# Attention heads of a two-model kernel: one by one, or in pairs on tiles of the matmul array

## The chip, the cores and the metric

One NeuronCore of a Trainium2 chip runs the whole program. Its engines are TensorE (PE, with its weight loads shown as PEld), VectorE (DVE), ScalarE (ACT), GpSimd (POOL) and the queue that issues the transfers (SP). The metric is the device time of one execution in microseconds; the kernel before has a median of 955.63 us over three runs (953.55 to 956.29).

## What is computed

The reference runs two small models on the same 256 tokens of width 1024: a retention layer and a sparse attention layer, then a second block. The change lies in that second block, after its input projection, where two mixers work side by side on 16 meta tokens and 256 real ones. The first is a gated delta rule (4 heads of 128) whose triangular systems are solved in chunks of 16, 128 and 128 tokens. The second is "forgetting" attention, 8 heads of width 64, each of which computes in fp32:

```
c  = cumsum(log_sigmoid(f_raw + f_bias))
sc = q @ k.T * 64**-0.5 + c[:, None] - c[None, :]     # 128 x 144 and 128 x 272 scores
p  = softmax(where(causal, sc, -1e30))
o  = p @ v
```

The outputs of the 256 real tokens alone are needed. Both mixers' outputs (512 columns each) then go through w_out and a SwiGLU layer.

## The kernel before, in words

Weights stream from HBM in units of 1 MB into a ring of four; ScalarE and VectorE split each into a high part (L1643) and a low part (L2082), and the projections take three matmul products of such parts. The mixers' own products (scores, values, triangular solves, transposes) are plain fp32 matmuls, which the trace shows as two passes for each instruction (all but the transposes); all of them are issued from line 776 (`mm`) or from lines of their own.

**The order.** `mixer_order()` is a list written out by hand. TensorE, VectorE and ScalarE each walk through it and do their share of every item, strictly in that order, so it also sets the order in which the four auxiliary PSUM banks are used: each use takes the bank of the use four places earlier (`Banks.open`), and waits until its reader has freed it. Items of the delta rule are `Lz` and `Lx` (level n of the triangular solve of chunk c: a product z and, above level 1, a transpose x; ScalarE copies z, VectorE copies x, and then a product y which VectorE subtracts from the matrix), `W`, and the recurrence over chunks `Vn` (new values), `Vo` (output and state) and `Vg` (norm and gate). GpSimd masks the rows for the next level (L2794) as soon as z of a level is there. `gz` and `mo` are projections with weights; `kv` and `vT` are transposes.

**One head of the forgetting attention** takes four items:
- `Fs`: `fox_scores` multiplies q (128 rows, of which the other head's 64 are zeros) by k, twice (144 and 272 columns), and adds the decay and the causal mask with bf16 products. VectorE takes the maxima (L2575, L2576), ScalarE the exponentials and sums into Pf (L2002), which frees the bank.
- `Fn`: VectorE inverts the sums and scales Pf (L2581, L2584).
- `Ft`: `fox_turn` turns Pf, three transposes of 128 columns (bank fT, copied by ScalarE at L2010) and two of 16 (bank fm, copied by VectorE at L2597).
- `Fo`: `fox_values` multiplies the values of both heads of a pair (128 columns, half of them unused) by the turned Pf in three products of 256, 256 and 128 columns. ScalarE rounds the 64 rows that count (L2015), VectorE subtracts for the low part (L2592), and that frees the bank.

The order puts the eight heads' items between the levels of the solve (`beside[n]`, one list behind the level's `Lz`, one behind its `Lx`), and the last ones (`Fs` of head 7, `Ft` of 6 and 7, `Fo` of 5, 6 and 7) between `W` and `Vn` of chunk 2.

## Time and profile before

| what | value |
|---|---|
| median of three runs | 955.63 us |
| the profiled execution's own time | 952.64 us |
| its span in the trace | 951.1 us |
| TensorE busy | 935.9 us (98%), 6542 passes |
| VectorE busy | 635.5 us (67%) |
| ScalarE busy | 478.5 us (50%) |
| GpSimd busy | 122.0 us (13%) |
| mixers with the attention heads | about 665 to 737 us of the span |

The span runs from the first to the last recorded instruction; the execution's own time is 1.5 us longer. "psum<-R,nw" names what an operation writes and reads: q of heads 0 to 3 lies in nw, of heads 4 to 7 in R; Pf and PfT are the probabilities and their turned form; G (G1 in the program's order), side_sb and PTb belong to the solve. "128*128 128x272 x2" is the part of the array used (rows * columns), the output, and the passes.

### The profile page before, as it was taken

To read this page: it belongs to the slowest core of one execution; us is meant where nothing else is said; L and a number is where in the kernel's file an instruction comes from. 1 tells how busy PE (TensorE), PEld (TensorE's weight loads), DVE (VectorE), ACT (ScalarE), POOL (GpSimd) and SP (SyncE) were. 2 spreads that over 40 slices of the span, in tenths; PEclk is the share of its full clock that TensorE was granted. 3 is DMA by queue.
4 is the path that set the end of the run, shared out by engine and by line. 5 is a ranking of instruction groups with operands and counts; after the bars stand their busy time and mean duration, and the time that the engine had idled before them with its cause. 6 is when DMAs were issued, how large, how long until landed. Compare 5 with 4: busy or idle time off the path is not lost.

```text
span 951.1 us, 16259 instructions
## 1 busy us (share of the span) xinstructions
PE 935.9 (98%) x6542; PEld 835.2 (88%) x6542; DVE 635.5 (67%) x942; ACT 478.5 (50%) x843; POOL 122.0 (13%) x128
## 2 busy tenths in 40 slices
PE   8999999999999999999999999999999999999997
PEld 8988778878998999998888789989788899999885
DVE  5974457566884767678874477988664667666543
ACT  7335446455654554466653556664434554444432
POOL 1000032000320000101310004312320111111001
PEclk9999999999999999999999999999999999999999
DMA  9735435555555863332025453522101555555551
GB/s 326 297 135 187 167 133 177 177 177 177 180 201 209 291 227 134 132 135 89 1 87 180 171 183 134 176 91 89 47 2 45 177 192 186 187 212 178 195 204 44
DMA packets 23518, 150.58 MB, mean 158 GB/s; under 512 B 3564, under 2 KB 3848, under 8 KB 6168
## 3 DMA queue, kind: packets, MB, share of 16 engines
q1 hardware_dynamic: 23104, 149.39, 44.7%
q8 instruction: 52, 0.85, 0.4%
q10 hardware_dynamic: 344, 0.18, 0.1%
q14 instruction: 18, 0.15, 0.1%
HBM read 148.50 MB, written 1.05 MB: 157 GB/s over the span
## 4 chain that ended last, share of the span: by engine, by line
PE 87%; DVE 7%; ACT 3%; issue 1%; DMA 1%; POOL 0%; SPq 0%; ACTq 0%; POOLq 0%; DVEq 0%
PE psum L776 83%; DVE ring_parts L2082 3%; PE psum L857 1%; DVE R L2407 1%; ACT high_parts L1643 1%; ACT R L1828 1%; PE psum L1190 1%; PE psum L1526 1%; DMA h<-in_x 1%; DVE R L2359 1%; DVE PTb_parts L2378 0%; ACT tmp L1681 0%; ACT R L1650 0%; PE psum L1373 0%; DVE nw_parts L2380 0%
## 5 line engine op out<-in xcount | busy, mean ns | idle before, releaser
L2082 DVE TENSOR_TENSOR ring_parts<-ring,high_parts 128x1024 fp32r<-128x1024 f32 (+1 forms) x272 | 333.3, 1264 | 146.4 <-ACT high_parts L1643 145.0
L1643 ACT CAST high_parts<-ring 128x1024 fp32r<-128x1024 f32 x268 | 268.1, 1050 | 185.7 <-PE psum L776 151.8
L776 PE MATMUL psum<-xT_parts,high_parts 128*128 128x256 f32 (+1 forms) x1024 | 228.0, 285 | 1.6 <-DVE ring_parts L2082 1.1
L776 PE MATMUL psum<-xT_parts,ring_parts 128*128 128x256 f32 (+1 forms) x704 | 200.6, 285 | 0.0
L776 PEld LDWEIGHTS psum<-xT_parts,high_parts 128*128 128x128 f32 x1024 | 173.3, 190 | 2.9 <-DVE ring_parts L2082 1.6
L776 PE MATMUL psum<-high_parts,R_parts 128*128 128x512 f32 (+1 forms) x528 | 164.8, 386 | 0.0
L776 PE MATMUL psum<-R_parts,high_parts 128*128 128x256 f32 x832 | 156.0, 277 | 0.0
L776 PE MATMUL psum<-high_parts,xT_parts 128*128 128x512 f32 x480 | 154.3, 397 | 0.0
L776 PEld LDWEIGHTS psum<-xT_parts,ring_parts 128*128 128x128 f32 x704 | 133.3, 189 | 0.1
L776 PEld LDWEIGHTS psum<-R_parts,high_parts 128*128 128x128 f32 x832 | 130.5, 188 | 0.0
L776 PEld LDWEIGHTS psum<-high_parts,R_parts 128*128 128x128 f32 (+1 forms) x528 | 98.7, 188 | 20.5
L776 PEld LDWEIGHTS psum<-high_parts,xT_parts 128*128 128x128 f32 x480 | 89.4, 188 | 20.9 <-issue 1.9
L776 PE MATMUL psum<-ring_parts,xT_parts 128*128 128x512 f32 x256 | 100.6, 393 | 0.0
L776 PE MATMUL psum<-ring_parts,R_parts 128*128 128x512 f32 (+1 forms) x264 | 99.3, 381 | 0.0
L776 PE MATMUL psum<-R_parts,ring_parts 128*128 128x256 f32 x352 | 97.2, 276 | 0.0
L776 PE MATMUL psum<-PTb_parts,high_parts 128*128 128x256 f32 x256 | 73.8, 288 | 0.0
L776 PEld LDWEIGHTS psum<-R_parts,ring_parts 128*128 128x128 f32 x352 | 66.1, 188 | 0.0
L776 PEld LDWEIGHTS psum<-ring_parts,R_parts 128*128 128x128 f32 (+1 forms) x264 | 49.6, 188 | 9.6
L776 PEld LDWEIGHTS psum<-ring_parts,xT_parts 128*128 128x128 f32 x256 | 48.1, 188 | 10.7
L776 PEld LDWEIGHTS psum<-PTb_parts,high_parts 128*128 128x128 f32 x256 | 48.3, 189 | 0.0
L776 PE MATMUL psum<-R 128*128 128x128 f32 (+3 forms) x248 | 47.2, 324 | 0.6 <-DVE R_parts L2592 0.6
L2757 POOL TENSOR_TENSOR R<-R,small 128x1024 f32<-128x1024 f32 x12 | 22.8, 1898 | 194.6 <-DVE small L2354 194.6
(354 smaller groups left out, 1126.4 us busy)
## 6 DMA issues: line engine op xcount, KB each, us to landing
ring<-in_weights SPq DMA_DIRECT2D x135, 1024.0 KB, 4.9
h<-in_x SPq DMA_DIRECT2D x4, 256.0 KB, 4.4
ring<-in_weights SPq DMA_DIRECT2D x4, 256.0 KB, 5.9
ring<-in_weights SPq DMA_DIRECT2D x2, 512.0 KB, 7.4
G<-in_gains SPq DMA_DIRECT2D x2, 512.0 KB, 7.7
out<-xn SPq DMA_DIRECT2D x2, 512.0 KB, 2.6
R<-in_ret_tabs SPq DMA_DIRECT2D x1, 768.0 KB, 13.0
tab<-in_tabs SPq DMA_DIRECT2D x1, 663.5 KB, 6.0
```

Of the source, the lines that this page charges most:

```text
L776: return pe.matmul(out, lhsT, rhs, start=first, stop=last, skip_group_check=True)
L857: ins = pe.transpose(bank[:, k * T + t * P:k * T + (t + 1) * P], src(2 * f + k, t), ident)
L1190: ins = pe.transpose(bank[:, n * P:(n + 1) * P], R[:, c0:c0 + P], ident)
L1526: ins = pe.transpose(bank[0:n, hd * n:(hd + 1) * n], mat(PTb, C_ALL, c, hd), ident[0:n, 0:n])
L1643: act.copy(as_r(hi), value).then_inc(sem("units_high"), 1)
L1828: ins = act.activation(R[:, c0:c0 + n_keys], bank[:, n * n_keys:(n + 1) * n_keys], ACT.Exp, bias=nmx[:, col:col + 1], accum_out=esum[:, co ...
L2082: return dve.tensor_tensor(as_r(value), value, value_of(hi), ALU.subtract)
L2359: main.free(dve.tensor_tensor(two(R[:, R4 + n * 512:R4 + (n + 1) * 512]), two(bank), token_scale2, ALU.mult), key)
L2407: ins = dve.scalar_tensor_tensor(y, raw[:, j, k:k + TM], param("conv_w_2", 12 * k + j), y, ALU.mult, ALU.add)
L2757: pool.tensor_tensor(p, p, spread(esc[:, i * 8:i * 8 + 2 * nh], 1024 // (2 * nh)), ALU.mult).then_inc(sem("nsa_p"), 1)
```

## The change

Heads are handled in pairs. `Fs`, `Fn`, `Ft` and `Fo` have the pair as their key, four of each in place of eight.

- Scores: q and k of one head are read from 64 partitions and not from 128, the two heads' from the lower and the upper half, so each pass takes 64 rows of the array (two row tiles, 64*128). The two heads' products are written in turn, each into a bank of its own; then each head gets its four bf16 products as before.
- Turning: both heads' three large transposes, each into its own bank, and four small ones into one bank. VectorE copies that bank once.
- Values: each product loads 64 columns of values and writes its head's 64 partitions of a common bank (two column tiles, 128*64), the two heads' products in turn. ScalarE and VectorE then handle all 128 partitions at once: four evictions each, where there were eight.
- The order is given anew: the pairs' items stand elsewhere between the levels, and at levels 1 to 3 the side work stands ahead of chunk 0's item and not behind it. `Fs`, `Ft` and `Fo` of the last heads no longer stand inside the recurrence.

```diff
-    beside = {1: ([("Fn", 0), ("vT", 1), ("Fs", 1)], [("vT", 2), ("vT", 0), ("Ft", 0)]), 2: ([("Fn", 1), ("Fs", 2)], [("Fo", 0), ("Ft", 1)]),
...
+              2: ([("Fs", 1)], [("Fo", 0), ("Fn", 1)]),
...
-    order += [("W", 1), ("Fs", 7), ("W", 2), ("Fo", 5), ("Vn", 0), ("Fn", 7), ("Ft", 6), ("Vo", 0), ("gz", 1, 1), ("Vn", 1),
-              ("Fo", 6), ("Ft", 7), ("Vo", 1), ("Fo", 7), ("Vg", 1), ("Vn", 2), ("mo", 0, 0), ("Vo", 2), ("Vg", 2),
...
+        for kind, side_work in zip(("Lz", "Lx"), beside[n]):
+            order += [(kind, n, c) for c in level_chunks(n) if c] + side_work + [(kind, n, c) for c in level_chunks(n) if not c]
+    order += [("W", 1), ("W", 2), ("Ft", 3), ("Vn", 0), ("Fo", 3), ("Vo", 0), ("gz", 1, 1), ("Vn", 1), ("Vo", 1), ("Vg", 1),
...
+            def fox_scores(pair):
+
+                banks = [aux.open(pe, ("fs", 2 * pair + i)) for i in range(2)]
+                k0 = R3 + 4 * TM + pair * TM
+                spans = ((0, P + M), (P + M, 2 * P + M))
+                for b, (c0, n) in enumerate(spans):
+                    for i in range(2):
+                        q = fox_query(2 * pair + i)[head_rows(i), b * P:(b + 1) * P]
+                        mm(banks[i][:, c0:c0 + n], q, R[head_rows(i), k0:k0 + n], b == 0, False)
...
+            def fox_values(pair):
+                wait_read(pe, aux, ("fT", 2 * pair + 1))
+                wait_read(pe, aux, ("fm", pair))
+                bank = aux.open(pe, ("fo", pair))
+                for c, (c0, n, at_) in enumerate(((384, T, 0), (0, T, 0), (T, P, P))):
+                    for i in range(2):
+                        v0 = R3 + 8 * TM + c * 512 + pair * P + i * FD
+                        ins = mm(bank[head_rows(i), at_:at_ + n], R[:, v0:v0 + FD],
+                                 PfT[:, i * 640 + c0:i * 640 + c0 + n], c == 0, c == 2)
+                aux.full(ins, ("fo", pair))
```

The whole list of `beside` is now: level 1, behind `Lz` Fn 0 and vT 1, behind `Lx` vT 2, vT 0 and Ft 0; level 2, Fs 1, then Fo 0 and Fn 1; level 3, gz (0, 0), then Ft 1; level 4, Fs 2, then Fo 1 and Fn 2; level 5, gz (0, 1), then Ft 2; level 6, Fs 3, then Fo 2, gz (1, 0) and Fn 3 (the numbers of F items are pairs). Pair 0's scores stand ahead of kv 0 as head 0's did. The VectorE and ScalarE parts follow the pairs in the same way (two heads' maxima, exponentials and scalings one after the other).

How instructions move, on TensorE at level 2. Before, from one head's scores to the first y products (side_sb,PTb) of the level:

```order
L776 MATMUL psum<-R,nw 128x144 [waits aux_read_by_act]
L776 MATMUL psum<-negc,of_head_3 128x144
L776 MATMUL psum<-causal_b,ident_b 128x128
L776 MATMUL psum<-R,nw 128x272
L776 MATMUL psum<-negc,of_head_3 128x272
L776 MATMUL psum<-causal_b,ident_b 128x128
L776 MATMUL psum<-side_sb,PTb 64x32 [waits aux_read_by_dve,aux_read_by_act]
L776 MATMUL psum<-side_sb,PTb 64x32 x7
L776 MATMUL psum<-side_sb,PTb 64x32 [waits aux_read_by_act,aux_read_by_dve]
L776 MATMUL psum<-side_sb,PTb 64x32 x7
```

Now, from the second head's mask products of pair 1 on:

```order
L774 MATMUL psum<-negc,of_head_3 128x144
L774 MATMUL psum<-causal_b,ident_b 128x128
L774 MATMUL psum<-negc,of_head_3 128x272
L774 MATMUL psum<-causal_b,ident_b 128x128
L774 MATMUL psum<-PTb,R 16x8 [waits aux_read_by_act,aux_read_by_dve,level_part]
L774 MATMUL psum<-PTb,R 16x8 x3
L1528 MATMUL psum<-tab,PTb 16x16 [waits aux_read_by_dve]
L1528 MATMUL psum<-tab,PTb 16x16 x3
L774 MATMUL psum<-side_sb,PTb 64x32 [waits aux_read_by_act,aux_read_by_dve]
L774 MATMUL psum<-side_sb,PTb 64x32 x7
L774 MATMUL psum<-side_sb,PTb 64x32 [waits aux_read_by_act,aux_read_by_dve]
L774 MATMUL psum<-side_sb,PTb 64x32 x7
```

Chunk 0's z and x (R 16x8 and 16x16) now stand between the scores and the y products, and two banks of scores are open where there was one; the first y product is the fourth use behind the first head's scores.

On VectorE, from level 2's subtractions (L2570, now L2573) to level 3's copies of x (L2564, now L2567). Before:

```order
L2570 TENSOR_TENSOR PTb<-PTb,psum 64x4x8x4 [waits aux_filled]
L2570 TENSOR_TENSOR PTb<-PTb,psum 64x4x8x4
L2570 TENSOR_TENSOR PTb<-PTb,psum 16x8x4 [waits aux_filled]
L2592 TENSOR_TENSOR R_parts_56<-psum,R_parts_56 64x256 [waits fox_high,aux_filled]
L2597 COPY PfT<-psum 16x256 [waits aux_filled]
L2564 COPY PTb<-psum 128x512 [waits aux_filled] x2
L2564 COPY PTb<-psum 16x64 [waits aux_filled]
```

Now:

```order
L2573 TENSOR_TENSOR PTb<-PTb,psum 64x4x8x4 [waits aux_filled]
L2573 TENSOR_TENSOR PTb<-PTb,psum 64x4x8x4
L2595 TENSOR_TENSOR R_parts_56<-psum,R_parts_56 128x256 [waits fox_high,aux_filled]
L2585 RECIPROCAL small<-small 128x2 [waits aux_read_by_act]
L2588 TENSOR_SCALAR Pf<-Pf,small 128x144 [waits dve_step]
L2588 TENSOR_SCALAR Pf<-Pf,small 128x272
L2585 RECIPROCAL small<-small 128x2 [waits aux_read_by_act]
L2588 TENSOR_SCALAR Pf<-Pf,small 128x144 [waits dve_step]
L2588 TENSOR_SCALAR Pf<-Pf,small 128x272
L2573 TENSOR_TENSOR PTb<-PTb,psum 16x8x4 [waits aux_filled]
L2567 COPY PTb<-psum 128x512 [waits aux_filled] x2
```

Chunk 0's subtraction (16x8x4) now stands behind the values' eviction and behind the scaling of two heads' probabilities, and so do the copies of x.

## Rows read from the trace of the kernel before

**Rows 1.** Windows: us; busy us and instructions of each engine; TensorE clock; DMA share; GB/s
```profile
690.00:710.00 20.00, 20.00 (x233) 17.13 (x232) 12.25 (x32) 8.01 (x24) 5.00 (x4) 1.00 0.01 2
770.00:800.00 30.00, 30.00 (x267) 30.00 (x266) 20.80 (x24) 14.64 (x17) 3.90 (x3) 1.00 0.55 191
```

**Rows 2.** Waits of TensorE from 664 to 740 us: us in total, times, longest
```profile
PE psum L776 <- DVE R_parts L2592: 0.6, 1, 0.6
PE psum L1452 <- ACT Pf L2002: 0.5, 1, 0.5
...
PE psum L776 <- DVE R L2534: 0.4, 1, 0.4
```

**Rows 3.** Timeline of TensorE, one head's scores and what follows (start us, us)
```profile
669.33 0.41 PE L776 MATMUL psum<-R,nw 128*128 128x144 f32 x2
669.58 0.23 PE L776 MATMUL psum<-negc,of_head 128*128 128x144 bf16 x1
...
669.70 0.68 PE L776 MATMUL psum<-R,nw 128*128 128x272 f32 x2
670.21 0.28 PE L776 MATMUL psum<-negc,of_head 128*128 128x272 bf16 x1
...
670.48 0.30 PE L776 MATMUL psum<-side_sb,PTb 64*64 64x32 f32 x4
```

**Rows 4.** Timeline of TensorE, one head's values and what follows
```profile
701.76 1.25 PE L776 MATMUL psum<-PfT,R 128*128 128x256 f32 x6
702.85 0.49 PE L1373 MATMUL psum<-tab,Pf 128*128 128x128 f32 x3
```

**Rows 5.** Timeline of TensorE in windows of 12 and 15 ns, and one row further on
```profile
666.60 0.27 PE L1335 MATMUL psum<-tab,R 128*16 128x128 f32 x1
666.81 0.24 PE L776 MATMUL psum<-PTb,G 64*64 64x32 f32 x1
...
675.13 0.25 PE L776 MATMUL psum<-PTb,G 64*64 64x32 f32 x2
...
675.72 0.66 PE L1526 MATMUL psum<-tab,PTb 128*128 128x128 f32 x4
```

**Rows 6.** Timeline of all engines, from a head's last score pass to its free bank
```profile
670.33 0.22 PE L776 MATMUL psum<-causal_b,ident_b 128*128 128x128 bf16 x1
...
671.33 0.38 ACT L2002 ACTIVATE Pf<-psum,small 128x144 f32<-128x144 f32 x1 [1.11 <-DVE small L2576]
...
672.42 0.52 PE L1452 MATMUL psum<-tab,tmp 128*128 128x128 f32 x3 [0.54 <-ACT Pf L2002]
```

**Rows 7.** Timeline of VectorE and GpSimd while both work from SBUF, and without GpSimd
```profile
667.62 2.49 POOL L2794 TENSOR_TENSOR G<-PTb,tab 128x512 f32<-128x512 f32 x2 [17.08 <-PE psum L776]
...
667.99 2.29 DVE L2584 TENSOR_SCALAR Pf<-Pf,small 128x144 f32<-128x144 f32 x2
...
677.33 0.56 DVE L2584 TENSOR_SCALAR Pf<-Pf,small 128x144 f32<-128x144 f32 x2
```

**Rows 8.** Timeline of all engines, the state's chain and the gate beside it
```profile
728.04 0.38 PE L776 MATMUL psum<-R,PTb 128*128 128x128 f32 x2
...
729.62 0.69 DVE L2508 SCALAR_TENSOR_TENSOR R<-tmp,R 128x512 f32<-128x512 f32 x1 [2.54 <-ACT tmp L1681]
...
729.82 1.25 PE L776 MATMUL psum<-PfT,R 128*128 128x256 f32 x6
730.02 0.58 ACT L2024 COPY R<-psum 128x512 f32<-128x512 f32 x1 [0.43 <-PE psum L776]
...
734.13 1.25 PE L776 MATMUL psum<-PfT,R 128*128 128x256 f32 x6
...
735.22 0.32 PE L776 MATMUL psum<-R,PTb 128*128 128x128 f32 x1
```

**Rows 9.** Lines by form: the eviction by VectorE of one head's values (count, busy us, mean ns)
```profile
L2592 DVE TENSOR_TENSOR R_parts<-psum,R_parts 64x256 fp32r<-64x256 f32 x8 | 3.4, 421 | 9.3 <-ACT R_parts L2015 7.3 <-PE psum L1377 2.0
```

**Rows 10.** Windows: a stretch in which the granted clock fell
```profile
649.70:653.30 3.60, 3.60 (x20) 3.60 (x19) 3.42 (x9) 0.77 (x1) 0.84 (x2) 0.55 0.00 0
```

More of the change, by code:

```diff
@@ L1380, in fox_values, with head_rows @@
[L1380 to L1393 removed]
+            def head_rows(i):
+                return slice(i * FD, (i + 1) * FD)
@@ new lines, in fox_scores @@
+            def fox_scores(pair):
[7 more added lines that the diff above has]
+                for i in range(2):
+                    hd = 2 * pair + i
+                    for c0, n in spans:
+                        mm(banks[i][:, c0:c0 + n], of_head_3[:, hd:hd + 1].to_broadcast([P, P]), negc[:, 0:n], False, False)
+                        ins = mm(banks[i][:, c0 + n - P:c0 + n], ident_b, causal_b, False, True)
+                    aux.full(ins, ("fs", hd))
@@ new lines, in fox_turn @@
+            def fox_turn(pair):
+                for i in range(2):
+                    hd = 2 * pair + i
+                    pe.wait_ge(sem("fox_scaled"), hd + 1)
+                    bank = aux.open(pe, ("fT", hd))
+                    for n, c0 in enumerate((M, P + 2 * M, 2 * P + 2 * M)):
+                        ins = pe.transpose(bank[:, n * P:(n + 1) * P], Pf[:, i * 416 + c0:i * 416 + c0 + P], ident)
+                    aux.full(ins, ("fT", hd))
+                bank = aux.open(pe, ("fm", pair))
+                for i in range(2):
+                    for n, c0 in enumerate((0, P + M)):
+                        ins = pe.transpose(bank[0:M, i * T + n * P:i * T + (n + 1) * P],
+                                           Pf[:, i * 416 + c0:i * 416 + c0 + M], ident)
+                aux.full(ins, ("fm", pair))
@@ L2006, in _ @@
-                    aux.free(ins, ("fs", hd))
+                    for i in range(2):
+                        hd = 2 * key[0] + i
+                        bank = aux.wait(act, ("fs", hd))
+                        act.wait_ge(sem("fox_max"), hd + 1)
+                        at_ = 0
+                        for b in range(TT):
+                            n = M + (b + 1) * P
+                            c0 = i * 416 + at_
+                            ins = act.activation(Pf[:, c0:c0 + n], bank[:, at_:at_ + n], ACT.Exp,
+                                                 bias=fnm[:, 2 * hd + b:2 * hd + b + 1],
+                                                 accum_out=fsum[:, 2 * hd + b:2 * hd + b + 1])
+                            at_ += n
+                        aux.free(ins, ("fs", hd))
@@ L2007, in _ @@
                 elif kind == "Ft":
-                    hd = key[0]
-                    bank = aux.wait(act, ("fT", hd))
-                    aux.free(act.copy(PfT[:, hd % 2 * 640:hd % 2 * 640 + 384], bank[:, 0:384]), ("fT", hd))
+                    for i in range(2):
+                        hd = 2 * key[0] + i
+                        bank = aux.wait(act, ("fT", hd))
+                        aux.free(act.copy(PfT[:, i * 640:i * 640 + 384], bank[:, 0:384]), ("fT", hd))
                 elif kind == "Fo":
-                    hd = key[0]
@@ L2013, in _ @@
-                    bank = aux.wait(act, ("fo", hd))
-                    p0 = hd % 2 * FD
-                    act.copy(as_r(fox_out_of(hd)[0]), bank[p0:p0 + FD, 0:T]).then_inc(sem("fox_high"), 1)
+                    pair = key[0]
+                    bank = aux.wait(act, ("fo", pair))
+                    act.copy(as_r(fox_out(pair)[0]), bank[:, 0:T]).then_inc(sem("fox_high"), 1)
                 elif kind == "W":
```

108 lines of the change are left out of this document (32 added, 76 removed), and 3 rows, old and new, of the table beside.

## The prediction

> **What bounds the kernel now.** I read the windows first. From 690 to 710 us TensorE is busy for all of the time while VectorE works 12 of 20 us and ScalarE 8, and later, in the SwiGLU, matmuls and weight loads both fill the window [rows 1]. So TensorE sets the time, in the mixers too, and a microsecond of its work taken away comes off the end unless TensorE waits for it instead. The list of waits says how far it is from that now: between 664 and 740 us it waited five times, for 2.2 us in all (0.6, 0.5 twice, of which one row stands, 0.4 and 0.2) [rows 2]. Everything behind the mixers keeps its work and its order, so what counts is when TensorE leaves the recurrence. I add up against the profiled execution (952.64 us) and carry the difference to the median (955.63 us).
>
> **Work that goes: scores.** One head takes 1.15 us of TensorE (669.33 to 670.48), of it 0.25 for the product of 144 columns and 0.51 for that of 272, the rest for four bf16 products [rows 3]. A pair takes 2.30. If the two row tiles run side by side, a pair takes 0.76 for both heads' products, 0.6 for eight bf16 ones and 0.2 for two changes of the tiles' shape, 1.56 in all: 0.74 less, four times, 3.0 us. The change of shape is priced from the pass of 128 rows that begins at 666.60: its kind follow each other every 0.11 us, the next pass, on 64*64, begins 0.21 later [rows 5], so 0.10. One that costs nothing would give 0.4 more back over the pairs, one of 0.3 would take 1.6.
>
> **Work that goes: values.** A head takes 1.09 us, a pair 2.18 [rows 4]. Side by side it is 1.09 and some 0.16 for changes of shape, 1.25: 0.93 less, four times, 3.7 us. Together 6.7 us.
>
> Do tiles run side by side? In the solve's products two passes of 64*64 are under way 15 ns after the first began [rows 5], while 256 columns take 0.22 us a pass (1.09 us for 640 columns in two passes each [rows 4]), which makes 27 ns for such a pass's 32 columns: two stream at once. Those tiles differ in rows and columns; the change's share the one or the other, which no row shows. Bounds: nothing gained (neither product shrinks, 7.4 us more than the sum below), or all of it. I take all, since the fp32 passes are of the same kind.
> The Trainium skill (TensorE: Matmul & The Clock Gate, Part 3) has 2.38 times for three column tiles and 3.07 for four row tiles, less than full. Two tiles at the same share, about 1.55 times, would be an estimate from that page of 2 us more than my sum, 959.2 us; the trace shows no such pair.
>
> **Evictions.** VectorE loses four of the eight values' subtractions of 0.42 us [rows 9], ScalarE four roundings, and half of the small copies merge. Neither engine sets the time, so this is worth nothing by itself. The transposes stay the same in number: nothing. No transfer is issued at another place.
>
> **Waits that go.** The five waits stood at places that the new order rearranges; I count them all as gone, 2.2 us, and price the new order's waits afresh.
>
> **Waits that come.** A bank of scores is free for TensorE 2.1 us after its head's last mask product (670.33 to 672.42), 1.1 us of it for the exponentials [rows 6], so the second head's bank comes 0.9 to 1.1 after the first's. Each auxiliary use takes the bank of four uses earlier, and a pair opens two score banks.
> - Level 1: z of chunks 1 and 2 take them. Between lie the other head's masks (0.3) and kv 0 (eight passes of 0.11, 0.9): 0.9 of wait, then 0.4. Behind it the pair's first turn needs subtractions that VectorE does after four scalings, of which two meet GpSimd's masking: two scalings took 2.29 us beside it and 0.56 without [rows 7]. That is 0.7 more. Sum 2.0.
> - Level 2: y of chunks 1 and 2 take the two banks. Between lie 0.3 of masks, 0.1 and chunk 0's z and x, 0.6: 1.1 of wait. The product itself takes 0.59 (16 passes, 675.13 to 675.72 [rows 5]), then 0.4 for the second. Sum 1.5. Before, z and x of the whole level lay ahead of the scores, and y had other banks.
> - Level 3: x of chunk 2 takes the bank of chunk 0's y, which VectorE frees behind the values' eviction and the scaling of two heads. After the values' end ScalarE needs 0.5, VectorE 0.5, the scalings 1.5, the small subtraction and its signal 0.3: 2.9. TensorE arrives after chunk 0's y, z, x and z at 0.59 each and 0.4: 2.2. So 0.7 at least. But GpSimd masks the next level's rows just then, and if each of its two operations holds back a scaling as in [rows 7], it is 2.8. I take 2.0, one of them caught and part of the other.
> - Level 4: the values' bank is the first score bank: 2.1 less 1.6 of masks and two y: 0.5. Level 5: the same collision delays VectorE, whose split of a weight half lies behind it: 0.5.
> - Behind the solve: pair 3's scaling stands behind the gate of gz. That ended 2.3 us after gz's last pass (728.04 to 730.31 [rows 8]); 0.75 and a signal later the first head is scaled, at 3.1. TensorE has two `W` of 0.9 (half of `Vn`, which takes 1.78 [rows 8]), so 1.3 of wait, and 0.4 for the second head. Sum 1.7.
> - In the recurrence: `Vo` 1 needs the new values copied, 0.9 us after `Vn` 1 (729.82 to 730.60 and a signal); `Vn` 2 needs the state, 1.1 us after `Vo` 1 (734.13 to 735.22) [rows 8]. Values and turns of heads 6 and 7 filled both; now nothing does. Sum 2.0.
>
> The waits come to 2.0 + 1.5 + 2.0 + 1.0 + 1.7 + 2.0 = 10.2 us. The sum: -6.7 - 2.2 + 10.2 = +1.3 us. The profiled execution would take 954.0 us, the median 956.9 us. With the unknown terms at their ends (level 3 at 0.7 or 2.8, changes of shape at 0 or 0.3) this case spans 955.2 to 959.3 us.
>
> What a measurement of this kernel tells from no change is about 0.3%, 2.9 us, so this is no change that can be told. The saved work is real, but it was what filled the solve's and the recurrence's waits.
>
> **Rival 1: the tiles do not run side by side.** The change then does not do what it says. Each product lasts as long as before, and 4 x (0.76 + 1.09) = 7.4 us stay: 964.3 us, slower. It decides once the second tile's pass starts only when the first has streamed. For it: half of the array's rows or columns are shared, and no row shows such a pair. Against it: [rows 5].
>
> **Rival 2: the waits are half of what I make them.** Each is worked out from an unhurried queue of VectorE and ScalarE. If the collisions with GpSimd don't happen (level 1, 3 and 5: 0.7, 1.3 and 0.5) and VectorE, relieved of 1.7 us of subtractions, comes earlier elsewhere, 5.1 us of waits remain: 951.8 us, faster. For it: in most levels before, GpSimd's masking fell beside copies from PSUM that it did not hold up.
>
> **Rival 3: the clock falls.** Once before, in 649.7 to 653.3 us, behind a stretch of small products, the granted clock was 0.55 in the mean, which is mostly the lower level of 1.2 GHz [rows 10]; 3.6 us at 0.55 cost 1.6 us against 2.4 GHz. The new order has waits of 1 to 3 us beside small products at levels 1 to 3. One or two such stretches: 958.5 to 960.1 us.
>
> **How the numbers follow.** My case has 0.50 (0.44 of it within 0.3%, 0.06 slower), rival 1 0.15 (slower), rival 2 0.17 (0.15 faster, 0.02 within), rival 3 0.18 (0.14 slower, 0.04 within). That makes 0.15 faster, 0.50 within, 0.35 slower. The time is my case's, 956.9 us. The range runs from rival 2's time, 951.8, to 961.5, above rival 3 and the upper end of my case; it leaves out rival 1 and half of rival 2's spread, about 2 in 10.
>
> **What would show it.** In the changed profile the list of waits of TensorE in the mixers would grow from 2.2 to about 10 us, with VectorE's scaling and its copy of x at level 3, the exponentials at levels 1, 2 and 4, the gate ahead of pair 3's turn, and the copies of new values and of the state as releasers. A pair's four score products would span about 0.8 us and its six of values 1.1 us from first start to the next form's; 1.5 and 2.2 would mean rival 1. Passes of the second tile would begin within some 10 ns of the first's. The clock's row would be 10 throughout but for that one dip; a second dip is rival 3. I am wrong if TensorE's waits stay below 6 us, or if it leaves `Vn` 2 more than 3 us away from where it does now.

## The result, and the profile after

The changed kernel takes 957.15 us (median of 22 runs, 953.81 to 967.96), the kernel before in the same series 955.42 us (22 runs, 951.70 to 957.73). The ratio is 1.0033, 95% interval 1.0016 to 1.0049. A second series later gave 958.44 against 955.84 us, ratio 1.0035 (1.0013 to 1.0057). The forecast was 956.9 us, within 0.3% of no change; the time fell on the forecast, some 2 us over the kernel before. How it came about is another matter, and the sections below take it apart: the number was met in part by luck.

| | before | changed |
|---|---|---|
| profiled execution | 952.64 us | 959.25 us |
| its span | 951.1 us | 957.6 us |
| its mean granted clock | 0.996 | 0.991 |
| first score pass to first pass of `Vn` 2 | 70.4 us (664.79 to 735.22) | 72.1 us (669.55 to 741.64) |
| of it TensorE idle | 2.4 us | 8.15 us |

The two profiled executions differ by 6.6 us, but 4.8 of these are there when the first scores begin, in parts that the change leaves alone (the input's transfer and a low clock behind it, a wait of 2.2 us near 650 that one execution has and another not, a granted clock of 0.83 in 630 to 640). I therefore compare the stretch from the first score pass to `Vn` 2, and call it **the segment**: it grew by 1.7 us; the sum of the prediction's terms was +1.3.

TensorE's list of waits in the changed kernel, 660 to 745 us (releaser, us in total, times, longest), which answers to [rows 2]:

```profile
PE psum L1528 <- DVE PTb L2573: 2.4, 1, 2.4
PE psum L774 <- ACT Pf L2005: 2.0, 3, 1.1
PE psum L1377 <- DVE Pf L2588: 1.1, 1, 1.1
PE psum L774 <- issue: 0.9, 1, 0.9
PE psum L774 <- ACT R L2027: 0.7, 1, 0.7
PE psum L774 <- DVE PTb L2573: 0.5, 1, 0.5
PE psum L774 <- ACT R L1995: 0.2, 1, 0.2
```

Five waits of 2.2 us have become nine listed ones of 7.8 us, with the releasers that the prediction named. (With gaps under 0.2 us the idle time is 8.15.) Windows of the same kernel (us; busy time and instructions of TensorE, its weight loads, VectorE, ScalarE, GpSimd; granted clock, DMA share, GB/s), for [rows 1, 10]:

```profile
650.00:660.00 10.00, 7.76 (x51) 7.26 (x48) 8.69 (x18) 2.07 (x5) 1.98 (x3) 0.83 0.02 6
670.00:680.00 10.00, 8.98 (x143) 6.98 (x140) 7.78 (x19) 6.99 (x25) 3.00 (x4) 1.00 0.01 2
680.00:690.00 10.00, 8.10 (x139) 6.14 (x137) 5.93 (x15) 3.45 (x14) 4.27 (x5) 1.00 0.02 4
690.00:700.00 10.00, 8.14 (x92) 6.72 (x94) 6.23 (x14) 2.08 (x4) 0.88 (x1) 0.83 0.30 105
700.00:710.00 10.00, 9.47 (x140) 7.62 (x137) 6.87 (x17) 4.59 (x14) 5.01 (x4) 1.00 0.01 2
```

In 690 to 710 TensorE was busy for all of the 20 us before; now it is for 8.1 and 9.5 of 10 each. And 690 to 700 has a granted clock of 0.83: a fall inside the mixers, for 3.4 us from 691.3, near the end of the longest wait (689.41 to 691.86). The kernel before has none from the first scores on; its one fall, near 650, lies ahead of the mixers, as three of this profile's four do.

TensorE's timeline over the first pair's scores (start, us, line and operation, out<-in, shape, count), for [rows 3]:

```profile
669.55 0.97 PE L774 MATMUL psum<-R,nw 64*128 64x144 f32 x8
670.45 0.24 PE L774 MATMUL psum<-negc,of_head 128*128 128x144 bf16 x1
...
671.04 1.04 PE L1333 MATMUL psum<-tab,R 128*16 128x128 f32 x8
672.79 0.30 PE L774 MATMUL psum<-PTb,G 64*64 64x32 f32 x4 [0.71 <-ACT Pf L2005]
```

The next passes follow the eight of both heads' products, in two row tiles, 0.90 us after those began, and the eight bf16 ones take 0.59: a pair takes 1.49 us (669.55 to 671.04) where two heads took 2.30. The last row is the first wait: z of level 1 wants the bank that ScalarE's exponentials still read.

The same kernel, all engines, from pair 0's values to the longest wait; for [rows 4, 7, 9]:

```profile
686.07 1.30 PE L774 MATMUL psum<-PfT,R 128*64 128x256 f32 x12
...
687.30 0.35 PE L774 MATMUL psum<-R,PTb 16*16 16x8 f32 x8
...
687.89 0.42 DVE L2595 TENSOR_TENSOR R_parts<-psum,R_parts 128x256 fp32r<-128x256 f32 x1 [1.13 <-ACT R_parts L2018]
...
688.40 2.49 POOL L2797 TENSOR_TENSOR G<-PTb,tab 128x512 f32<-128x512 f32 x2 [4.61 <-DVE R_parts L2595]
688.42 2.62 DVE L2588 TENSOR_SCALAR Pf<-Pf,small 128x144 f32<-128x144 f32 x2
...
688.76 0.66 PE L774 MATMUL psum<-PTb,G 64*64 64x32 f32 x16
...
691.15 0.57 DVE L2588 TENSOR_SCALAR Pf<-Pf,small 128x144 f32<-128x144 f32 x2
691.63 0.17 DVE L2573 TENSOR_TENSOR PTb<-PTb,psum 16x32 f32<-16x32 f32 x1
...
691.86 0.47 PE L1528 MATMUL psum<-tab,PTb 128*128 128x128 f32 x1 [2.45 <-DVE PTb L2573]
```

Six column-tiled products (twelve passes, each on 64 columns of the array) take 1.23 us (686.07 to 687.30) where a pair took 2.18; one subtraction of 128x256 takes 0.42 us, as one of 64x256 did. Then the collision: two scalings that take 0.57 us alone take 2.62 beside GpSimd's 2.49; level 2's small subtraction, queued behind four scalings, ends at 691.8, and TensorE stands for 2.45 us.

The end of the solve and the recurrence; for [rows 8]:

```profile
727.41 1.22 PE L1377 MATMUL psum<-tab,Pf 128*128 128x128 f32 x6 [1.06 <-DVE Pf L2588]
727.46 0.56 DVE L2588 TENSOR_SCALAR Pf<-Pf,small 128x144 f32<-128x144 f32 x2
...
728.47 0.60 PE L1382 MATMUL psum<-tab,Pf 128*16 128x128 f32 x4
...
737.80 2.05 PE L774 MATMUL psum<-R 128*128 128x128 f32 x16 [0.68 <-ACT R L2027]
...
741.64 0.46 PE L774 MATMUL psum<-R,PTb 128*128 128x128 f32 x2 [0.90 <-issue]
```

Pair 3's turn waits 1.06 us for the first head's scaling (and takes 1.06 instead of 0.72 since the second head's comes late); `Vo` 1 waits 0.68 for the copy of the new values, `Vn` 2 0.90. The profile names no releaser for the last; it is the state by its time, since VectorE's update of it (L2611) runs from 740.85 to 741.54, 0.10 ahead of `Vn` 2.

Summed over the segment, each pass counted from its start to the next one's: values 9.06 to 4.93 us, scores and masks 9.10 to 6.17, idle time 2.38 to 8.15, turns 4.83 to 5.54, the gates' products and the transposes of x, some of them at the lower clock, 1.2 more. The rest of the difference, 1.0 us, is spread over a dozen forms with 0.07 to 0.26 each and I did not trace it further.

### The profile page after: what moved, and what is told of

It reads as the page before. It is cut to its first block, busy times and chain, and to the rows that moved or that the text cites. A ratio compares the mean times of both kernels' runs of the same rounds, so it can differ in the third digit from the quotient of the medians.

```text
span 957.6 us, 16243 instructions
## 1 busy us (share of the span) xinstructions
PE 935.6 (98%) x6542; PEld 832.4 (87%) x6542; DVE 636.3 (66%) x934; ACT 477.1 (50%) x839; POOL 121.4 (13%) x128
## 4 chain that ended last, share of the span: by engine, by line
PE 86%; DVE 7%; ACT 3%; issue 1%; DMA 1%; POOL 0%; SPq 0%; ACTq 0%; POOLq 0%; DVEq 0%
PE psum L774 82%; DVE ring_parts L2085 3%; PE psum L855 1%; DVE R L2410 1%; ACT R L1830 1%; PE psum L1188 1%; ACT high_parts L1645 1%; DMA h<-in_x 1%; PE psum L1528 1%; DVE R L2362 1%; DVE PTb_parts L2381 0%; DVE Pf L2588 0%; ACT tmp L1683 0%; PE psum L1377 0%; ACT Pf L2005 0%
## 5 line engine op out<-in xcount | busy, mean ns | idle before, releaser
L774 PE MATMUL psum<-R 128*128 128x128 f32 (+4 forms) x248 | 46.4, 333 | 0.7 <-ACT R L2027 0.7
```

Of the source, the lines that this page charges most:

```text
L774: return pe.matmul(out, lhsT, rhs, start=first, stop=last, skip_group_check=True)
```

## What the runs' clock tells

Each run has a mean granted clock, and the time follows it. The 105 runs of the kernel before that were taken beside the experiments (median 955.1 us) have a mean of 0.996, and 32 of them 0.999, which leaves room for some 2 us at the lower of its two levels (1.2 and 2.4 GHz) in the whole run; the profiled execution, with the one fall of [rows 10], has 0.996. The changed kernel's 34 runs (median 957.7) have 0.992, and none has 0.999. A straight line through each kernel's runs (0.75 to 0.85 us for 0.001 of clock) gives at the same clock of 0.995 955.4 us before and 955.6 changed. So **at one clock the two kernels are the same, and the 2 to 3 us between the medians are a clock that is lower more often**. Below, "at 0.995" is such a line through the kernel's own runs; with 12 runs it is good to about 1 us (the four series of the kernel before, of 23 to 35 runs, give 954.9 to 955.7), and worse with the 6 or 7 runs of two experiments.

The mean does not say where the clock fell. Of the changed kernel's profile 13.7 us are at the lower level, but 10.3 of them ahead of the first scores, where both kernels do the same work; its second profile, shown further down, has none there and 6.8 us in the segment. The segment's share, 3.4 and 6.8 us in two profiles against nothing in the one of the kernel before, is what the change can have brought.

## Experiments

No kernel leaves work out; each edit is against the changed kernel.

**Row tiles off.** The scores read all 128 rows, the rest is as changed.

```
-  q = fox_query(2 * pair + i)[head_rows(i), b * P:(b + 1) * P]
-  mm(banks[i][:, c0:c0 + n], q, R[head_rows(i), k0:k0 + n], b == 0, False)
+  q = fox_query(2 * pair + i)[:, b * P:(b + 1) * P]
+  mm(banks[i][:, c0:c0 + n], q, R[:, k0:k0 + n], b == 0, False)
```

> The changed kernel with the scores' query and key read from all 128 rows again (the other head's rows of the query are zero), all else as changed: same order, same evictions, values still in two column tiles. My theory (the tiles run side by side and lie on TensorE's path): the pair's eight products of 64x128 by 64x144 and 64x272, 0.90 us in the changed kernel's trace, take 1.5 to 1.65 us, so a pair of scores goes from 1.49 to about 2.2; four pairs are 2.8 us, of which 0.5 to 1.0 may vanish in waits that follow (the bank wait of 0.71 and 1.11 us behind pairs 1 and 2). From the first scores to the third chunk's value correction (72.1 us now) it takes 74 to 75 us; the kernel is 2.0 to 2.8 us slower than the changed one, so 3.5 to 4.5 us over the kernel before. Rival (the work that the tiles save is off the path, in waits for other engines anyway): the segment stays at 72.1 within 0.5 us, and so does the time. Rival (tiles not side by side): the eight products take 0.9 us as they do now.

Measured: 959.74 us (7 runs), ratio to before 1.009 (1.0056 to 1.0124), mean clock 0.989; 954.9 at 0.995. Its timeline:

```profile
663.72 1.57 PE L774 MATMUL psum<-R,nw 128*128 128x144 f32 x8
665.13 0.23 PE L774 MATMUL psum<-negc,of_head 128*128 128x144 bf16 x1
...
665.71 0.49 PE L1333 MATMUL psum<-tab,R 128*16 128x128 f32 x3
```

The eight products take 1.41 us against 0.90, 0.51 more, not 0.6 to 0.75. So the tiles are worth 0.49 a pair, 2.0 us in all four. The scores and masks took 9.1 us before, 8.15 here and 6.2 in the changed kernel: 0.95 of what the change saved on them was never the tiles', but comes from handling two heads at once. A pair goes back from bf16 to fp32 passes once less for each head (0.06 us each time), and its passes stand fewer times beside passes of another tile shape (0.09 to 0.10 each).

The segment is 72.9 us, only 0.8 longer than in the changed kernel's first profile: the 2.45 us wait is missing here, and the clock was low for 6.8 us from 681 on instead of 3.4 from 691. So the expectation of 74 to 75 failed, by a thing that is explained further down. The changed kernel's second profile is the fairer partner, with the same waits (5.7 us of idle time) and as long a stretch of low clock: its segment is 71.1, so 1.75 us are lost here, about what the tiles are worth. The line at 0.995 doesn't show that: it has this kernel 0.7 us under the changed one. It rests on seven runs and is steeper (1.09 us for 0.001) than the others, and I trust the segment more.

**Column tiles without alternation.** The values' products head by head.

```
-  for c, (c0, n, at_) in enumerate(((384, T, 0), (0, T, 0), (T, P, P))):
-      for i in range(2):
+  for i in range(2):
+      for c, (c0, n, at_) in enumerate(((384, T, 0), (0, T, 0), (T, P, P))):
```

> The changed kernel with the values' products of a pair issued head by head (all of the first head's columns, then all of the second's) instead of in turns between the two column tiles. Same products, same tiles, same order otherwise. If two column tiles overlap only when neighbours in the issue order lie in different tiles, a pair of values goes from 1.23 us back to about 2.0 to 2.2 us, four pairs are 3 to 3.8 us, the segment of 72.1 us becomes 75 to 76, and the kernel is 3 us slower than the changed one. If the tiles overlap whatever the issue order (queued per tile), the pair stays at 1.2 to 1.4 us and the time where it is. I take the first.

Measured: 959.07 us (12 runs), ratio 1.0062 (1.003 to 1.0093); 957.5 at 0.995, 1.9 over the changed kernel. TensorE's timeline over the first pair of values:

```profile
683.71 1.78 PE L774 MATMUL psum<-PfT,R 128*64 128x256 f32 x12
685.43 0.35 PE L774 MATMUL psum<-R,PTb 16*16 16x8 f32 x8
```

A pair takes 1.72 us: between the 1.23 of alternating heads and the 2.18 of before. Four pairs are 1.9 us, and the segment is 74.0, 1.9 longer, with the same idle time and as much low clock as in the changed kernel: what the tiles save here comes off the end one for one. The second head's first pass begins 0.49 us after the first head's, behind two of its six; from there on, until the first is through, a pass of the one begins 6 to 57 ns from a pass of the other. Neither of the two expected values came: without alternation about half of the gain is still there.

**Both off.**

> Both undone together (scores from 128 rows, values head by head), so what is left of the change is the new order, one eviction and one set of waits per pair. My theory: the tiles save 6.7 us of TensorE time in the segment and the new order gives back some 8 us as waits; with the tiles gone the segment of 72.1 us becomes 77.5 to 79 us (some of the bank waits, 0.7 and 1.1 us, are filled by the longer products), and the kernel takes 5 to 6.5 us more than the changed one, so about 6 to 8 us more than the kernel before. If the two prices overlap in the same waits, it is under 4 us. If the difference of 1.7 us between before and changed came from the clock and not from waits, this kernel is at most 4 us over the kernel before.

Measured: 961.28 us (6 runs), ratio 1.0078 (1.0054 to 1.0102); 959.6 at 0.995, 4.0 over the changed kernel. The segment is 77.1 us, 5.0 longer: 2.0 and 1.9 for the tiles, the rest a stretch at the lower clock that is twice as long (690 to 700 at 0.66 in place of 0.83). The idle time is 8.15 us again, wait by wait: the longer products filled none of it. So the two savings add up, are real, and lie on the path.

**Pair 1's scaling behind level 2.**

```
-  2: ([("Fs", 1)], [("Fo", 0), ("Fn", 1)]),
-  3: ([("gz", 0, 0)], [("Ft", 1)]),
+  2: ([("Fs", 1)], [("Fo", 0)]),
+  3: ([("Fn", 1), ("gz", 0, 0)], [("Ft", 1)]),
```

> The changed kernel with one entry moved: the scaling of pair 1's exponentials goes from the end of level 2 to the head of level 3's first side, ahead of the first z-gate. In the changed kernel VectorE has these four scalings ahead of level 2's last subtraction, they take 2.62 us each twice beside a GpSimd operation of 2.49, and TensorE waits 2.4 us for that subtraction, after which the granted clock of 690:700 is 0.83. My theory: the 2.4 us wait goes (under 0.6 left), the clock of 690:700 is 0.95 or more, and the segment of 72.1 us is 2.5 to 4 us shorter; the kernel is 2 to 4 us faster than the changed one and at or under the kernel before. Rival (the wait only moves): the scalings meet the GpSimd operations at the new place too, the next level's subtraction or the transposes of pair 1 wait 1.5 us or more, and the segment is within 1 us of 72.1. Rival (clock is chance): the 2.4 us go but the clock falls elsewhere, and the time is no better than 1.5 us.

Measured: 955.66 us (12 runs), ratio 1.0033 (1.0009 to 1.0058), mean clock 0.992; 954.0 at 0.995, 1.6 under the changed kernel. Windows of its profile:

```profile
650.00:660.00 10.00, 8.96 (x47) 8.46 (x48) 7.37 (x18) 2.10 (x5) 0.66 (x1) 0.66 0.01 2
...
690.00:700.00 10.00, 10.00 (x142) 7.83 (x141) 7.21 (x19) 2.83 (x6) 3.39 (x3) 1.00 0.32 107
```

The wait of 2.45 us is gone without a successor, the clock of 690 to 700 is full, and the segment is 68.3 us: 2.5 us less by the wait and 1.3 by the clock. But the mean clock of the 12 runs is no better than the changed kernel's (0.992 both), and one profile with a full clock in the segment doesn't say how often that happens; the falls of this profile, in 630 to 640 and 650 to 660, lie ahead of the mixers, where the changed kernel's has two as well.

**The wait filled.** The same products once more, to keep TensorE busy ahead of its wait.

```
   bank = aux.open(pe, ("z", lv, c))
-  for hd in range(GH):
+  for hd in list(range(GH)) * (5 if (lv, c) == (3, 2) else 1):
```

> The changed kernel with one thing added and nothing moved: the 16 products of level 3's z for the second chunk are computed five times in place of once, each time over the same result, so that TensorE works 2.4 us more just ahead of its wait of 2.45 us for VectorE's subtraction. Nothing is left out of the computation. If the fall of the granted clock behind the wait (0.83 in 690:700) comes from TensorE having stood idle, then the wait is under 0.3 us, the clock of the stretch behind it is 0.97 or more, the segment from first scores to Vn2 falls from 72.1 to 70.3 to 71 us although TensorE does more work, and the kernel is no slower, perhaps 1 us faster. If the clock falls for another reason (such as the work being done at the time, or chance), the stretch behind still shows 0.85 or less in the profile and the segment stays at 72.1 within 0.4. If the added products delay ScalarE's eviction and with it the level, the segment grows by up to 2.4 us.

Measured: 956.41 us (12 runs), ratio 1.0013 (0.9985 to 1.0041); 955.3 at 0.995. Windows of its profile:

```profile
680.00:690.00 10.00, 8.69 (x183) 7.01 (x181) 6.42 (x19) 2.67 (x12) 2.71 (x3) 1.00 0.01 2
690.00:700.00 10.00, 10.00 (x135) 7.99 (x132) 5.69 (x12) 3.21 (x7) 3.78 (x3) 1.00 0.31 107
```

The timeline of VectorE and GpSimd in it:

```profile
687.21 1.60 DVE L2588 TENSOR_SCALAR Pf<-Pf,small 128x144 f32<-128x144 f32 x2
...
690.23 1.29 POOL L2797 TENSOR_TENSOR G<-PTb,tab 128x512 f32<-128x512 f32 x1 [1.77 <-DVE PTb L2567]
```

The added products take 1.9 us (z takes 2.45 in place of 0.6), the wait of 2.45 is gone, and the segment is 70.1 us, 2.0 shorter than the changed kernel's: 1.4 of it is the clock, which stays full. The edit did more than fill the wait: z is copied later, so GpSimd's second operation begins at 690.2, behind the scalings, and holds up none; the first two scalings take 1.60 us and not 2.62.

That the clock fell because TensorE stood idle fits this profile, and two of the twelve runs have a mean clock of 0.999, which none of the changed kernel's 34 has. It is not shown: over all twelve the mean is 0.992, as in the changed kernel, and four are at 0.990 and below.

**The levels' order anew.** Pair 1's scores and scaling move into level 3, pair 2's into level 5, values ahead of the scores; the end stays (the new end is in the next kernel, both are in the one after).

```
-  2: ([("Fs", 1)], [("Fo", 0), ("Fn", 1)]),
-  3: ([("gz", 0, 0)], [("Ft", 1)]),
-  4: ([("Fs", 2)], [("Fo", 1), ("Fn", 2)]),
-  5: ([("gz", 0, 1)], [("Ft", 2)]),
-  6: ([("Fs", 3)], [("Fo", 2), ("gz", 1, 0), ("Fn", 3)])}
+  2: ([], [("Fo", 0)]),
+  3: ([("Fs", 1), ("gz", 0, 0), ("Fn", 1)], [("Ft", 1)]),
+  4: ([("Fo", 1)], []),
+  5: ([("Fs", 2), ("gz", 0, 1), ("Fn", 2)], [("Ft", 2)]),
+  6: ([("Fo", 2)], [("Fs", 3), ("Fn", 3), ("gz", 1, 0)])}
```

> The new order's levels with the changed kernel's end (from W on as changed). Prices the first half: of the changed kernel's idle time, the waits of 0.71, 1.11, 2.45 and 0.53 us in the levels should go (4.8 us), those of 1.06, 0.68 and 0.90 behind W stay. Segment from first scores to Vn2: 72.1 less 4 to 5 and less about 1.5 of the slow clock, so 66 to 67.5 us; kernel 3 to 5 us faster than the changed one at the same clock, if the waits don't just move. If VectorE sets the pace, segment 68 to 69.

Measured: 958.47 us (12 runs), ratio 1.0037 (1.0014 to 1.006), mean clock 0.988. The idle time fell to 5.3 us, but the segment is 77.9 us, over ten more than expected: the granted clock is 0.66 in 670 to 680, 0.83 in 690 to 700 and in 700 to 710, 0.68 in 710 to 720 and 0.81 in 720 to 730. At 0.995 the kernel is at 954.3, 1.3 under the changed one.

**A new end.** `Vn` 0 ahead of pair 3's turn, pair 3's values between `Vn` 1 and `Vo` 1, two products of the output around `Vn` 2, pair 3's scaling ahead of the last gate.

```
-  6: ([("Fs", 3)], [("Fo", 2), ("gz", 1, 0), ("Fn", 3)])}
+  6: ([("Fs", 3)], [("Fo", 2), ("Fn", 3), ("gz", 1, 0)])}
-  order += [("W", 1), ("W", 2), ("Ft", 3), ("Vn", 0), ("Fo", 3), ("Vo", 0), ("gz", 1, 1), ("Vn", 1), ("Vo", 1), ("Vg", 1),
-            ("Vn", 2), ("mo", 0, 0), ("Vo", 2), ("Vg", 2), ("H", 0), ("mo", 0, 1), ...
+  order += [("W", 1), ("W", 2), ("Vn", 0), ("Ft", 3), ("Vo", 0), ("gz", 1, 1), ("Vn", 1), ("Fo", 3), ("Vo", 1), ("Vg", 1),
+            ("mo", 0, 0), ("Vn", 2), ("mo", 0, 1), ("Vo", 2), ("Vg", 2), ("H", 0), ...
```

> The changed kernel's levels with the new end (Vn0 ahead of pair 3's turn, pair 3's values between Vn1 and Vo1, two output products around Vn2) and pair 3's scaling ahead of the last z-gate's low parts on VectorE. Prices the second half: the waits of 1.06, 0.68 and 0.90 us should go or fall under 0.3 each, 2 to 2.6 us in all, while 2.45 us in level 3 and the clock step behind it stay. Kernel 1.5 to 2.6 us faster than the changed one at the same clock. Rival (these three are floors of the recurrence's own chain through ScalarE and VectorE and only change place): under 0.8 us.

Measured: 954.20 us (12 runs), ratio 0.9997 (0.9973 to 1.0021); 952.0 at 0.995, 3.6 under the changed kernel, where 1.5 to 2.6 was expected. All three waits behind `W` (1.06, 0.68, 0.90) are gone from its list, 2.6 us, and so is the slow second half of pair 3's turn, 0.3; the remaining 0.7 is within what the line can tell.

**Both together, the whole new order.**

> The changed kernel's tiles and evictions, with the table of the order written anew. Levels: pair 1's scores move from level 2 into level 3 with the first z-gate and then the scaling behind them; the values of pair 1 come ahead of the scores of pair 2, which move to level 5 in the same way; values of pair 2 into level 6's first side, scores of pair 3 and their scaling behind it. End: Vn0 ahead of pair 3's turn, pair 3's values between Vn1 and Vo1, the output's first two products on each side of Vn2. Theory (the tiles' saving is real and the order gave it back as waits): of the 8.15 us that TensorE idles between the first scores and Vn2 in the changed kernel, 1.5 to 3 are left; that segment (72.1 us; 70.4 in the kernel before; 68.3 with the scaling late) comes to 65.5 to 67.5 us, but two products of the output (about 2.8 us) are then inside it, so 68.5 to 70.5 by the clock on the wall, with the end of the program 4 to 6 us earlier than the changed kernel's at the same granted clock: 950 to 952 us at a mean clock of 0.995, where the changed kernel has 955.6 and the kernel before 955.3. Rival (VectorE sets the pace of the levels, so that the waits only move): 4 us or more of idle time are left, and the kernel is within 2 us of the one with the late scaling, 952 to 954 at 0.995. Rival (clock): the idle goes, but the mean clock falls by 0.003 or more below the changed kernel's 0.992 and the median does not follow.

Measured: 959.33 us (12 runs), ratio 1.0037 (1.0014 to 1.0061), mean clock 0.986; 951.2 at 0.995. Windows of its profile:

```profile
687.00:690.00 3.00, 2.10 (x48) 1.69 (x47) 2.45 (x8) 0.53 (x2) 0.00 (x0) 1.00 0.56 238
690.00:693.00 3.00, 2.67 (x29) 2.03 (x31) 2.09 (x8) 0.96 (x2) 0.00 (x0) 0.53 0.00 0
693.00:696.00 3.00, 3.00 (x31) 2.54 (x30) 0.69 (x1) 0.74 (x2) 1.71 (x2) 0.50 0.02 5
711.00:714.00 3.00, 1.75 (x23) 1.17 (x20) 2.87 (x11) 0.71 (x2) 0.00 (x0) 1.00 0.00 0
714.00:717.00 3.00, 2.95 (x16) 2.65 (x14) 0.92 (x2) 0.62 (x2) 0.00 (x0) 0.52 0.00 0
```

The third of my expectations came: the idle time is down to 3.5 us, at the same clock the kernel is 4.4 us faster than the changed one, and the clock takes it all back. It fell to its lower level twice, each time behind a wait of pair 1's or 2's turn for its scaling (0.88 and 0.34 us from 688.6, 1.13 us at 711.4), and stayed there for some 17 and 7 us. None of its runs has a mean clock over 0.993, so its 951.2 lies a little beyond what was measured. The first gate's twelve large passes (684.0 to 687.0) came just ahead of the first of these waits and did not keep it up.

**The two orders that paid.** The late scaling and the new end.

> The changed kernel with the two orders that paid: pair 1's scaling at the head of level 3 (scaling_late) and the new end with pair 3's scaling ahead of the last z-gate's low parts (tail_only). Theory: the two are worth 1.7 and 3.7 us at a mean clock of 0.995 against the changed kernel's 955.6, and touch different waits, so 950 to 951 us at that clock; idle time of TensorE from first scores to Vn2 3.0 us (0.71, 0.18, 1.11, 0.20, 0.53, some of 0.1), no granted clock under 0.95 between 670 and 740. Median 951.5 to 953, that is 0.3 to 0.5% under the changed kernel and 0.2 to 0.4% under the kernel before. Rival (the clock takes back what the waits give): mean clock under 0.990 and median 954 or more, as with the new order of the levels, whose idle time fell from 8.15 to 5.3 us and whose clock fell to 0.5 of full in three stretches.

Measured: 953.58 us (12 runs), ratio 0.9984 (0.996 to 1.0009), mean clock 0.991; 950.8 at 0.995, as expected. The idle time is 2.84 us, the waits that are left are level 1's, level 2's and level 4's; the clock fell again, to 0.77, 0.84 and 0.71 in the three windows from 670 to 700. The median missed its range by 0.6 us through the clock.

**And two fillers more.** The edit is against the kernel of both orders.

```
-  ("kv", 1), ("fv", 3), ("kv", 2), ("Fs", 0), ("kv", 0)
+  ("kv", 1), ("fv", 3), ("Fs", 0), ("kv", 2), ("kv", 0)
-  2: ([("Fs", 1)], [("Fo", 0)]),
+  2: ([("Fs", 1), ("Fo", 0)], []),
```

> The kernel called both_orders, with pair 0's scores one step earlier (ahead of the third chunk's key and value turns) and pair 0's values right behind pair 1's scores instead of behind level 2's second products, so that each pair's first exponentials have 1.0 to 1.2 us of other TensorE work beside them. If the waits of 0.71 and 0.18 (level 1) and of 1.11 and 0.20 us (level 2) are ScalarE's exponentials holding the banks, level 1's go and level 2's fall to some 0.8: 1.2 to 1.4 us less idle time than in both_orders, and 0.8 to 1.5 us less at the same clock. Rival: pair 0's scores wait for the log sums' transfer instead, or the values' bank waits for level 2's copies: within 0.5 us of both_orders.

Measured: 951.92 us (12 runs), ratio 0.9974 (0.9949 to 1.0000); 949.4 at 0.995, 1.4 under the kernel without them. TensorE's list of waits, 662 to 745 us:

```profile
PE psum L1333 <- ACT Pf L2005: 0.7, 1, 0.7
PE psum L774 <- ACT Pf L2005: 0.7, 1, 0.7
PE psum L1377 <- DVE PTb L2573: 0.6, 1, 0.6
PE psum L774 <- DVE PTb L2573: 0.5, 1, 0.5
```

Level 1's wait for the exponentials moved to `kv` 2 (0.71) instead of going, level 2's fell from 1.31 to 0.83, and pair 0's turn now waits 0.59. The idle time did not fall (3.0 us), so the 1.4 us at the same clock are not the idle time that I expected them to be. Where they come from is open; they are about what such a line can tell (the same kernel, run again below, is at 949.9).

**The changed kernel and the last one, once more.**

> The changed kernel unaltered, for a second profile. If the wait of 2.45 us in level 3 belongs to the order (VectorE's four scalings meeting GpSimd's operation), it is there again within 0.1 us, with idle time of TensorE from first scores to Vn2 of 8.1 to 8.2 us; the clock may fall elsewhere, and the segment is 70.7 to 72.4 us, by the clock. If the wait came by chance, the idle time is 6 us or less. Median 955 to 958.5, mean clock 0.991 to 0.994.

> The kernel both_orders_plus unaltered, beside the changed kernel on one chip. Median 951 to 953, 4 to 6 us under the changed kernel's; idle time 3.0 us again; mean clock 0.990 to 0.995.

Measured: 958.44 us for the changed kernel, ratio 1.0035 (1.0013 to 1.0057), and 953.84 for the other, ratio 0.9975 (0.9947 to 1.0004), 12 runs each. At 0.995 they are at 955.4 and 949.9. The second profile of the changed kernel was the surprise: its idle time is 5.7 us, and the wait of 2.45 us is not there. Its windows at that place:

```profile
680.00:682.00 2.00, 2.00 (x27) 1.35 (x26) 0.57 (x2) 0.37 (x1) 0.00 (x0) 0.74 0.00 0
682.00:684.00 2.00, 2.00 (x24) 1.60 (x24) 1.87 (x6) 0.37 (x1) 1.00 (x1) 0.50 0.03 8
684.00:686.00 2.00, 2.00 (x21) 1.94 (x21) 1.36 (x5) 0.37 (x1) 1.23 (x2) 0.50 0.00 0
```

and all engines over the same stretch:

```profile
681.78 1.06 PE L774 MATMUL psum<-PTb,G 64*64 64x32 f32 x16
...
682.59 0.57 DVE L2588 TENSOR_SCALAR Pf<-Pf,small 128x144 f32<-128x144 f32 x2
...
682.89 0.37 ACT L1995 COPY side_sb<-psum 128x256 f32<-128x256 f32 x1 [0.94 <-PE psum L774]
683.00 1.27 POOL L2797 TENSOR_TENSOR G<-PTb,tab 128x512 f32<-128x512 f32 x1 [5.27 <-PE psum L774]
...
683.26 1.37 DVE L2588 TENSOR_SCALAR Pf<-Pf,small 128x144 f32<-128x144 f32 x2
...
684.56 0.17 DVE L2573 TENSOR_TENSOR PTb<-PTb,psum 16x32 f32<-16x32 f32 x1
...
684.82 0.69 PE L1528 MATMUL psum<-tab,PTb 128*128 128x128 f32 x2
```

Here the clock fell at 681, behind the waits for the exponentials (1.11 and 0.20 us from 677.5). At the lower level the 16 products of z took 1.06 us in place of 0.65, so z was copied later, GpSimd's masking began later, and the first two scalings ran alone (0.57 us); then the subtraction ended ahead of TensorE. The profile of the kernel without row tiles shows the same pattern. So the order has two courses in the profiles: either the clock falls ahead of level 3's wait, or it stays up, VectorE and GpSimd collide, and it falls near the wait's end (the changed kernel's first profile and three of the experiments'). What decides between them no profile shows. The segment is 71.1 us in the one, 72.1 in the other.

## Why the prediction was right, and where it was not

**The work that goes** was right. A pair of scores takes 1.49 us (forecast 1.56), a pair of values 1.23 (1.25), 7.0 us saved in all against 6.7. Rival 1 is refuted. But 0.95 of the scores' 2.9 us come from handling two heads at once, and not from the row tiles, as the first experiment shows. The changes of shape were priced rightly at 0.10: the first bf16 pass behind a tiled one starts late by 0.09.

The estimate from the Trainium skill (TensorE: Matmul & The Clock Gate, Part 3), two tiles at 1.55 times, is not borne out by the column tiles: a pair of values took 2.18 and now 1.23 us, 1.77 times with the changes of shape in it. The row tiles' eight products look like it, 1.41 against 0.90 us or 1.57 times, but 0.19 of the 0.90 are two changes of shape; the passes alone run two at once in nearly the time of one.

**The waits that come** were the term that was mis-sized, in sum 8.7 us against 10.2 (8.15 of idle time, the rest turns that were drawn out). By place, measured (forecast): level 1 1.3 (2.0), level 2 1.3 (1.5), level 3 2.45 (2.0), level 4 0.5 (0.5), level 5 0.1 (0.5), pair 3's turn 1.4 (1.7), recurrence 1.6 (2.0). GpSimd held up scalings in level 1 too (one took 1.37 us, two more 1.45), but the turn behind them lost only 0.4 us; in level 3 both of pair 1's first scalings were caught. Most places were a little smaller than forecast; that I added each chain's parts end to end may be why, which no run singles out. The size of level 3's wait is that of one course only: in the second profile it is missing, and the sum is 6.2. The waits that went, 2.4 against 2.2, were right.

**The sum without the clock** is therefore -7.0 - 2.4 + 8.7 = -0.7 us, and not +1.3. Another 1.0 us, the part spread over a dozen forms, was in no term; with it the sum is +0.3, and the runs at one clock say +0.2. On this alone the change would have come out level.

**Rival 3 is the larger part of what made up the difference.** It had a chance of 0.18 and was held apart from my case; it should have been a part of it. Half clock behind level 3's wait cost 1.3 us in the segment (the difference between the wait's 2.5 us and the 3.8 us that removing it gave), and the mean clock over the runs is lower by 0.004. The number 956.9 was met by luck, because errors cancelled: waits 1.5 us too long on one side, on the other no clock in the central case (1.3) and 1.0 us of drawn-out passes that nobody had counted.

The prediction said it would be wrong with `Vn` 2 more than 3 us from its place; it began 6.4 us later, but 4.8 of that came from ahead of the scores, which the criterion did not allow for. Its other sign, waits that stay below 6 us, is met by the second profile (5.7 us of idle time) and not by the first (8.15): of the forecast 10 us of waits, 2.45 are there in one course and not in the other. It also spoke of one fall of the clock as normal; 32 of 105 runs of the kernel before have a mean of 0.999, which leaves no room for one of 3.4 us.

Some of its sums are off, none enough to change the forecast. Changes of shape that cost nothing would give back 0.8 us on the scores (eight changes at 0.10), not 0.4, so its own case begins at 954.8 us and not at 955.2. The parts of level 3's chain add up to 2.8, not 2.9. Its upper end of 2.8 for that wait does not follow from [rows 7]: 2.29 less 0.56 is 1.7, and 0.7 more is 2.4, which is what was measured. Two tiles at 1.55 times would make 959.1, not 959.2.

## What to carry to other kernels

Work that fills waits is not free to remove: working in pairs took 7 us off TensorE and the order that came with it handed back nearly all of it, while the same pairs with pair 3's and pair 1's fillers put elsewhere (and two more moved) came out at 951.92 and 953.84 us, ratio 0.9974 and 0.9975 to the kernel before. The intervals of both just reach 1.000, so even this gain is small against the spread. When a step is made shorter, write the order anew from the waits that remain, and look first for an engine that queues a freeing operation behind work nobody needs yet.

Compare kernels at the same granted clock as well as by the median: here the spread by clock (953.8 to 968.0 us for one kernel) is larger than what any edit did, and a new order with less idle time than any before it (3.5 against 8.15 us) gained nothing, as the clock was at its lower level for some 24 us of it.

## What was not expected of the hardware

- Two column tiles overlap in part even when one head's three products are issued before the other's: 1.72 us a pair, against 1.23 in turns and 2.18 untiled. The second tile's first pass begins 0.49 us after the first's, behind two of its six.
- A fall of the granted clock can begin behind waits of 0.7 to 1.3 us among small products, not only at one of 2.4 (the shortest: 0.69 and 0.14 us from 680.7, the fall at 683.0, in the kernel with two fillers more); and not every such wait brings one (in the changed kernel's first profile the clock was full through the waits at 672.8 and 684.6, in its second it fell behind the latter).
- VectorE's scaling from SBUF beside GpSimd: 1.33 and 1.37 us for operations of 0.30 and 0.35. Each began 25 to 50 ns behind an operation of GpSimd of 1.27 us and ended 90 to 160 ns behind it, as if it had waited for it. VectorE's copies from PSUM are not held up: 0.69 us at 688.85 in the kernel with the late scaling, beside GpSimd's operation from 688.38 to 689.65.
- Going back from bf16 to fp32 passes costs 0.06 us: behind a bf16 pass the next fp32 pass of 272 columns is followed by its second 0.285 us later, in the grouped order 0.229. The other way it costs nothing that shows (0.122 us from the last fp32 pass of 144 columns to the bf16 one, as between fp32 passes).
